# Filter stage, norms, recurrence and routing reordered in a three-block network on one core

## The chip, the cores and the metric

One core of a Trainium2 chip (trn2) runs the whole program once. The time is the device time of that execution in microseconds. The core has five engines that run their own instruction streams and wait for each other by semaphores: TensorE (PE in the rows, its weight loads PEld), VectorE (DVE), ScalarE (ACT), GpSimd (POOL) and SyncE (SP), which here only sends the DMA transfers. TensorE's clock has two levels, 2.4 and 1.2 GHz; the share of the first that was granted stands in the rows as PEclk.

## What is computed

Everything is float32, for 256 tokens of width 1024. Two layers (feed-forward, mixer, feed-forward; the mixers are attention and RWKV-7) are followed by a block with a Hyena and an HGRN2 mixer and a mixture of 16 experts. Each sublayer begins with a norm, modulated by a shift and a scale that come from a conditioning vector:

```python
y = xf * rsqrt(mean(xf * xf, axis=-1) + EPS) * g     # rmsnorm, per token
h = y * (1 + scale) + shift                          # modulate
x = x + factor * gate * _swiglu(h, w_in, w_out)      # silu(h @ w_gate) * (h @ w_up) @ w_down
# second block
h, hc = modulate(rmsnorm(x, g1), ..), modulate(rmsnorm(ctx, g1), ..)
p, pc = h @ w_in, hc @ w_in
y_hy = hyena_mixer(p[..., :1536], ..)     # z = x1 * (h1 conv v); y = x2 * (h2 conv z), filters by their frequencies
y_hg = hgrn_mixer(p[..., 1536:], pc[..., 1536:], ..)
#   S_t = diag(f_t) S_{t-1} + k_t v_t^T,  o_t = S_t^T q_t, both directions, start states from the context
x = x + g1 * concat([rmsnorm(y_hy), readout(y_hg)]) @ w_out
h2 = modulate(rmsnorm(x, g2), ..)
aff = softmax(h2 @ router_w)              # each expert takes its 32 best tokens
x = x + g2 * ec_moe(h2, router_w, w1, w3, w2)        # (silu(xg @ w1) * (xg @ w3)) @ w2, times the gate, added back
return rmsnorm(x, final_g)
```

## The kernel before

**Layout.** Activations lie transposed: 8 tiles of 128 features by 256 tokens (`x3`, `h3`, `sq3`). A float32 matmul is two rows of the trace.

**Norm.** ScalarE squares `x` in four pieces (L1386). TensorE multiplies a 128x128 matrix of ones with each of the eight tiles of squares (L664), so that PSUM bank 7 holds every token's sum in all 128 partitions, and then runs `busy` dummy matmuls on zeros (`keep_clock`, L659). VectorE turns the sums into variances over 128x256 (L1728), ScalarE takes the root (L1374), VectorE the reciprocal (L1724), and eight products with the scale follow (L1731); ScalarE adds the shift (L1391). The norms are numbered: 0 to 5 in the two layers, 6 is the final norm of the first block, 7 and 8 are those of `x` and of the context in the second, 9 is the one ahead of the routing. Norm 0 is special: the first 16 rows of the modulation are dot products on VectorE (`first_dots`, L1757) with weights that are loaded at the start, and GpSimd makes the normalised `x` (L1688).

**Order.** Every engine's program is written out by hand, in the order of the network. SyncE's list is fixed too: a load is sent when the semaphore of its place in the buffer allows, and what stands behind it in the list waits with it. Feed-forward groups are loaded one ahead (gate, up and down weights, 1 MB each), mixer weights go through a ring of four slots of 1 MB (`load`, L592).

**Filter stage.** The frequencies of two Hyena filters are five groups of matmuls each (`filter_freq`, L1039 to L1043) on sums and differences of the two filter sides, which VectorE makes (`filter_sides`) into one pair of buffers; it then empties the banks (`filter_end`, L2079 to L2083). TensorE's order is norm 6, filter 0, norm 7, filter 1, then `b2_in`: 20 of the 22 units of the input projection (L1071, L1069; a unit is 32 rows), with the Hyena convolutions between them. The last two units are cut into pieces of eight rows that `beside(i)` puts between steps of the recurrence (L1084), as it does with the Hyena half of the output projection (L1095).

**Recurrence.** `hgrn` does the scan by doubling: after `level` (L1123, eight matmuls for a direction) at block size 2^lev VectorE `taken`s the new part of the score matrix under a mask (L2126, L2129: two passes of 128x512), scales queries and keys (L2141, L2142) and updates the decays (L2147, L2148). There are eight rounds of two directions, called half levels here. Ahead of it stand turning the Hyena result (`hyena_back`, L1205), turning the context keys (L1108) and the context states (L1115); behind it the crossing between the two token halves (L1143), a last product (L2151), the output sums (L1151 to L1157), their norm, and the rest of the output projection (`b2_out`, L757).

**Routing and experts.** TensorE computes logits (L1215), turns them, the tokens and the affinities, and spreads each expert's row of affinities over 128 partitions (`spread`, L1238). VectorE ranks every token of an expert (`select`, L2222, L2224) and makes the picking matrix of the expert's 32 tokens (`pick`); TensorE gathers them (`picked`, L1247). An expert's weights are 12 loads of 2 MB, 192 in all, through nine places; place n is free when `moe_slot` says so. Loads 2 to 5 wait for the end of the output sums (`hg_out`), load 7 for the output projection, load 8 for the turned tokens, load 9 for the first slot's matmuls:

```python
            sp.wait_ge(sem("hg_out"), 2)
            for n in range(2, 6):
                expert_load(n)
```

## Time and profile before

| | us |
|---|---|
| median of 3 runs | 2678.49 (2677.92 to 2680.62) |
| the profiled execution | 2676.36 |
| its span, first to last instruction | 2674.3 |
| TensorE busy | 2302.1 (86%) |
| VectorE busy | 774.6 (29%) |
| ScalarE busy | 344.9 (13%) |
| chain that ended last: TensorE, DMA, VectorE | 62%, 30%, 7% |
| DMA traffic | 709.51 MB |

The rows come from one profiled execution; times in them count from the start of its span. The chain is followed back from the last instruction through whatever released each step. A busy TensorE is not always on it: in the experts it is busy beside the transfers. Matmuls overlap, so the mean time of one is longer than its share of a group.

### The profile page before, as it was taken

The numbers are of one execution on the slowest core, as the hardware profiler recorded it, in microseconds if no ns is written. First come the engines' busy times: TensorE is split into PE (matmuls) and PEld (weight loads), VectorE is DVE, ScalarE is ACT, GpSimd is POOL, SyncE is SP. The second block draws the span as 40 slices with busy tenths as digits, with TensorE's granted clock in tenths as the row PEclk, the third lists the DMA queues.
The fourth block names the chain that finished last, engine by engine and source line by source line (L and its number), as shares of the span: only waits on it lengthen the run. The fifth ranks groups of instructions, "written<-read, shape, count | busy, mean of one in ns | idle before, by whom it ended". The sixth has DMA issues, their size and how long they took to land.

```text
span 2674.3 us, 34093 instructions
## 1 busy us (share of the span) xinstructions
PE 2302.1 (86%) x14956; PEld 1619.0 (61%) x14968; DVE 774.6 (29%) x1473; ACT 344.9 (13%) x618; POOL 17.5 (1%) x21
## 2 busy tenths in 40 slices
PE   7999989999999999999999999896666666666675
PEld 5888768888888789888886878652121111111221
DVE  5544534574000465511023338640000000000000
ACT  3001222002000232111002211210000000000000
POOL 1000000000000000000000000000000000000000
PEclk9999999999999999999999999988887788887778
DMA  9889235886445240044442223489999999999997
GB/s 394 343 354 379 95 142 226 354 341 256 157 141 204 90 147 20 24 169 148 136 172 78 66 77 115 189 330 428 428 427 428 426 428 427 428 427 427 426 428 338
DMA packets 70098, 709.51 MB, mean 265 GB/s; under 512 B 7776, under 2 KB 7904, under 8 KB 8672
## 3 DMA queue, kind: packets, MB, share of 16 engines
q1 hardware_dynamic: 69984, 707.79, 65.6%
q8 instruction: 96, 1.57, 0.2%
q14 instruction: 18, 0.15, 0.0%
HBM read 706.71 MB, written 1.05 MB: 265 GB/s over the span
## 4 chain that ended last, share of the span: by engine, by line
PE 62%; DMA 30%; DVE 7%; ACT 1%; issue 1%; SPq 0%; DVEq 0%; ACTq 0%
DMA arena<-in_experts 27%; PE ps L691 11%; PE ps L698 11%; PE ps L708 11%; PE ps L757 5%; PE ps L875 4%; PE ps L1071 4%; PE ps L1282 2%; PE ps L1314 2%; DMA ring<-in_experts 2%; PE ps L664 1%; PE ps L1069 1%; PE ps L773 1%; PE ps L1247 1%; PE ps L787 1%
## 5 line engine op out<-in xcount | busy, mean ns | idle before, releaser
L1282 PE MATMUL ps<-arena 128*32 128x512 f32 x1376 | 211.8, 748 | 147.0 <-DMA arena<-in_experts 146.5
L691 PE MATMUL ps<-hT_sq,arena 128*128 128x256 f32 x1376 | 312.1, 380 | 4.1 <-ACT hT_sq L1391 2.9
L708 PE MATMUL ps<-hid,arena 128*128 128x256 f32 x1408 | 311.1, 379 | 0.2 <-DVE hid L1796 0.2
L698 PE MATMUL ps<-hT_sq,arena 128*128 128x256 f32 x1376 | 311.0, 379 | 0.0
L708 PEld LDWEIGHTS ps<-hid,arena 128*128 128x128 f32 x1408 | 267.4, 190 | 36.9 <-issue 0.6
L691 PEld LDWEIGHTS ps<-hT_sq,arena 128*128 128x128 f32 x1376 | 260.5, 190 | 45.5 <-issue 8.5
L698 PEld LDWEIGHTS ps<-hT_sq,arena 128*128 128x128 f32 x1376 | 261.4, 190 | 35.5
L1282 PEld LDWEIGHTS ps<-arena 128*32 128x32 f32 x1376 | 42.4, 124 | 310.6 <-DMA arena<-in_experts 226.0
L1363 ACT ACTIVATE arena<-ps 128x512 f32<-128x512 f32 (+4 forms) x147 | 89.1, 615 | 946.1 <-PE ps L1293 308.5
L1796 DVE TENSOR_TENSOR hid<-sil,ps 128x256 f32<-128x256 f32 x88 | 37.0, 421 | 560.4 <-ACT sil L1415 560.2
L1757 DVE CUSTOM_DVE_ANT_0 hT_sq<-arena 128x1024 f32<-128x1024 f32 x168 | 194.5, 1221 | 0.0
L2249 DVE TENSOR_TENSOR arena<-arena,ps 128x512 f32<-128x512 f32 x16 | 11.0, 688 | 552.4 <-PE ps L1282 552.4
L1314 PE MATMUL ps<-arena 128*32 128x512 f32 x688 | 108.7, 767 | 36.5 <-DMA arena<-in_experts 33.1
L1415 ACT ACTIVATE sil<-ps 128x256 f32<-128x256 f32 x88 | 33.7, 383 | 779.3 <-PE ps L698 778.9
L1282 PE MATMUL ps<-ring,arena 128*32 128x512 f32 x512 | 79.3, 751 | 48.3 <-DMA ring<-in_experts 48.3
L757 PE MATMUL ps<-arena,ring 128*128 128x256 f32 x512 | 111.5, 379 | 2.6 <-DVE arena L1894 1.8
L757 PEld LDWEIGHTS ps<-arena,ring 128*128 128x128 f32 x512 | 97.1, 190 | 17.6 <-DVE arena L1894 2.3
L2256 DVE TENSOR_TENSOR arena<-ps,arena 128x512 f32<-128x512 f32 x16 | 11.1, 692 | 306.4 <-PE ps L1314 306.4
L875 PE MATMUL ps<-arena 64*64 64x64 f32 x2848 | 85.9, 218 | 3.0 <-ACT arena L1363 2.1
L875 PEld LDWEIGHTS ps<-arena 64*64 64x64 f32 x2848 | 84.4, 135 | 3.8 <-ACT arena L1363 2.5
L1314 PEld LDWEIGHTS ps<-arena 128*32 128x32 f32 x688 | 22.4, 128 | 105.7 <-DMA arena<-in_experts 49.0
L1071 PE MATMUL ps<-hT_sq,ring 128*128 128x256 f32 x384 | 83.9, 379 | 0.0
(370 smaller groups left out, 2184.0 us busy)
## 6 DMA issues: line engine op xcount, KB each, us to landing
arena<-in_experts SPq DMA_DIRECT2D x129, 2048.0 KB, 41.1
arena<-in_ada SPq DMA_DIRECT2D x96, 1024.0 KB, 9.7
ring<-in_experts SPq DMA_DIRECT2D x42, 2048.0 KB, 40.9
ring<-in_ring_w SPq DMA_DIRECT2D x51, 1024.0 KB, 5.1
arena<-in_ffn_gate SPq DMA_DIRECT2D x44, 1024.0 KB, 6.5
arena<-in_ffn_up SPq DMA_DIRECT2D x44, 1024.0 KB, 6.2
arena<-in_ffn_down SPq DMA_DIRECT2D x44, 1024.0 KB, 4.8
hT_sq<-in_experts SPq DMA_DIRECT2D x21, 2048.0 KB, 40.4
```

Of the source, the lines that this page charges most:

```text
L691: last = mm(ps[:, ft, 0:T], gate3[:, kt, ft * P:(ft + 1) * P], h3[:, kt, :], start=kt == 0, stop=kt == KT - 1)
L698: last = mm(ps[:, ft, T:2 * T], up3[:, kt, ft * P:(ft + 1) * P], h3[:, kt, :], start=kt == 0, stop=kt == KT - 1)
L708: last = mm(acc(m), down3[:, ft, m * P:(m + 1) * P], hid3[:, ft, :], start=False, stop=True, skip_group_check=True)
L757: last = mm(out_of(m), slot(seq0 + kt // 2)[:, (kt % 2) * D + m * P:(kt % 2) * D + (m + 1) * P], rhs3[:, kt, :], start=(kt == 0 and m % 2 ...
L875: last = mm(ps[r, bank, kt * HD:(kt + 1) * HD], lhs[r, kt, :], rhs[r, :] if len(rhs.shape) == 2 else rhs[r, kt, :], start=start and (stop ...
L1071: last = mm(o, w[:, kt, j * P:(j + 1) * P], src[:, kt, :], start=kt == 0, stop=kt == KT - 1)
L1282: last = mm(ps[32 * n:32 * n + 32, part, :], e_xe[:, kt, :], w[:, (kt % 2) * SLOT + n * 512:(kt % 2) * SLOT + (n + 1) * 512], start=kt == ...
L1314: last = mm(ps[q:q + 32, 3, :], e_hT[:, i, 32 * n:32 * n + 32], w[:, i * D + nn * 512:i * D + (nn + 1) * 512], start=n == 0 and i < 2, sto ...
L1363: return f(dst, src, ACT.Copy)
L1415: f(sil3[:, ft, :], ps[:, ft, 0:T], ACT.Silu).then_inc(sem("silu_ready"), 1)
L1757: nc.vector.tensor_tensor_reduce(buf[:, out_at * D:(out_at + 1) * D], w, c_rows[:, which * D:(which + 1) * D], 1.0, 0.0, ALU.mult, ALU.add ...
L1796: tt_(hid3[:, ft, :], sil3[:, ft, :], ps[:, ft, T:2 * T], ALU.mult).then_inc(sem("hid_ready"), 1)
```

## The change

It has four parts.

1. *Norms.* The sum is made with the tokens on the partitions: each 128x128 piece of squares is the weights, one column of ones moves, and the sums are 128x2. Variance, root and reciprocal run on 128x2. `widen` then multiplies the broadcast column with the identity, which gives every token's factor in all partitions, and the products read it from PSUM. The dummies are split around `widen`. Norms 6 to 8 have none; there `widen` stands inside the filter groups and between projection units. At the start `x`, the vectors and the constants are loaded ahead of the conditioning row, and VectorE makes the normalised `x`, between the first dot products and the rest.
2. *Filters.* Both filters get their own sides, made ahead of the first group's end; the banks are emptied first and the biases added later.
3. *Recurrence.* `hyena_back` moves ahead of the last unit in `b2_in`; the first levels stand ahead of the turned context keys and the states; level 0 needs no scaled keys; the takes of levels 6 and 7 are block copies on ScalarE; pieces of `beside` move behind the levels, into the crossing and the output norm.
4. *Routing.* Only two experts are spread ahead of the first expert and fourteen behind its first four slots; the affinities are copied ahead of the tokens; dummies stand in the gaps; the tables of Exp and Sqrt are loaded early.

The core of the diff:

```diff
-            def norm(i, busy=0):
+            def norm(i, busy=(0, 0)):
+                if i == 7:
+                    pe.wait_ge(sem("x_ready"), 7 * KT)
                 for kt in range(KT):
                     pe.wait_ge(sem("squares"), 4 * i + kt // 2 + 1)
-                    last = mm(norm_sums(i), ones, sq3[:, kt, :], start=kt == 0, stop=kt == KT - 1)
+                    for tt in range(TT):
+                        last = mm(norm_sums[:, tt:tt + 1], sq3[:, kt, tt * P:(tt + 1) * P], ones[:, 0:1],
+                                  start=kt == 0 and tt == 0, stop=kt == KT - 1, skip_group_check=True)
                 last.then_inc(sem("norm_sum"), 1)
-                keep_clock(6, busy)
+                if busy:
+                    keep_clock(6, busy[0])
+                    widen(i)
+                    keep_clock(6, busy[1])
+
+            def widen(i):
+
+                pe.wait_ge(sem("norm_unit"), i + 1)
+                for tt in range(TT):
+                    last = mm(norm_wide[:, tt * P:(tt + 1) * P], norm_unit[:, tt:tt + 1].to_broadcast([P, P]), ident,
+                              start=True, stop=True)
+                last.then_inc(sem("norm_wide"), 1)
...
-                inverse_root(ts(rstd[:, :], norm_sums(i), 1.0 / D, EPS, ALU.mult, ALU.add), rstd[:, :])
+                root(ts(norm_unit, norm_sums, 1.0 / D, EPS, ALU.mult, ALU.add))
+                nc.vector.reciprocal(norm_unit, norm_unit).then_inc(sem("norm_unit"), 1)
+                dve.wait_ge(sem("norm_wide"), i + 1)
...
-            sp.dma_start(c_rows[:, 0:D], a["c_rows"][:, 0:D]).then_inc(sem("c_landed"), 16)
-            first_rows(0, 1)
-            start()
-            first_rows(1, 3)
+            start()
+            sp.dma_start(c_rows[:, 0:D], a["c_rows"][:, 0:D]).then_inc(sem("c_landed"), 16)
+            first_rows(0, 3)
...
-            norm(1, 20)
+            norm(1, (5, 8))
...
-            norm(6, 11)
+            norm(6, None)
             filter_freq(0)
-            norm(7)
+            norm(7, None)
+            keep_clock(0, 5)
             filter_freq(1)
             b2_in()
-            hyena_back()
             hgrn()
             b2_out()
-            norm(9, 10)
+            norm(9, (5, 3))
...
             norm(6, x3, x3, v("final_g", 0, 8), name="x_ready")
             scale_of(144 + 8, v("norm1_g", 0, 8))
+            filter_sides(1)
             filter_end(0)
             norm(7, x3, h3, coef[:, 0:8])
             filter_end(1)
+            filter_bias()
...
+                        if lev < MASKED:
+                            taken(lev, d)
+                        else:
+                            dve.wait_ge(sem("hg_level"), 2 * lev + d + 1)
...
+                for lev in range(MASKED, NLEV + 1):
+                    hb = 1 << lev - 1
+                    for d in range(2):
+                        act.wait_ge(sem("hg_level"), 2 * lev + d + 1)
+                        for tt in range(TT):
+                            src = ps[:, 4 + 2 * d + tt, :].rearrange("p (h s) -> p h s", s=P)
+                            for lo in range(0, P, 2 * hb):
+                                early, late = (slice(lo + hb * i, lo + hb * (i + 1)) for i in ((0, 1) if d == 0 else (1, 0)))
+                                last = copy(g_A[early, d, tt, :, late], src[early, :, late])
+                        last.then_inc(sem("hg_copied"), 1)
...
+                keep_clock(7, 2)
+                pe.wait_ge(sem("e_rows"), 3)
+                spread(range(0, 2))
+                keep_clock(7, 12)
                 pe.wait_ge(sem("e_rows"), 4)
-                spread(range(0, 8))
...
                         if e == 0 and part == 0:
-                            spread(range(8, NE))
+                            spread(range(2, NE))
```

TensorE from the last projection unit into the recurrence. Before, L1205 turns the Hyena result, L1108 the context keys, L1115 is the states, L1123 the levels, L1084 the pieces beside:

```order
L1069 MATMUL ps<-ring,arena 128x256 x16
L1205 MATMUL ps<-con,arena 128x128 x8
L1108 MATMUL ps<-con,arena 128x128 x16
L1084 MATMUL ps<-hT_sq,ring 128x256 x4
L1115 MATMUL ps<-arena 128x128 x16
L1084 MATMUL ps<-hT_sq,ring 128x256 x4
L1123 MATMUL ps<-arena 128x128 x24
L1084 MATMUL ps<-hT_sq,ring 128x256 x4
```

The same stretch of the changed kernel: L1233 turns the Hyena result, L1147 the context keys, L1135 is the states, L1125 the levels, L1103 the pieces beside:

```order
L1233 MATMUL ps<-con,arena 128x128 x8
L1088 MATMUL ps<-ring,arena 128x256 x16
L1125 MATMUL ps<-arena 128x128 x16
L1147 MATMUL ps<-con,arena 128x128 x16
L1125 MATMUL ps<-arena 128x128 x8
L1135 MATMUL ps<-arena 128x128 x8
L1125 MATMUL ps<-arena 128x128 x8
L1135 MATMUL ps<-arena 128x128 x8
L1125 MATMUL ps<-arena 128x128 x8
L1103 MATMUL ps<-hT_sq,ring 128x256 x4
```

The Hyena result is turned one unit earlier, the first levels lead, and the states stand where the first pieces beside stood.

TensorE from the end of the recurrence to the output projection, before (L1143 crossing, L1151 to L1157 output sums, L1163 their mean squares, L659 dummies):

```order
L1123 MATMUL ps<-arena 128x128 x8
L1095 MATMUL ps<-hT_sq,ring 128x256 x4
L1143 MATMUL ps<-arena 128x128 x8
L1151 MATMUL ps<-arena,sil 128x256
...
L1163 MATMUL ps<-hT_sq,con 128x512 x2
L659 MATMUL ps<-zeros 128x512 x8
L757 MATMUL ps<-hT_sq,ring 128x256 x32
```

And now (L1167 crossing, L1177 to L1186 output sums, L1191 mean squares, L1115 pieces beside, L770 output projection):

```order
L1125 MATMUL ps<-arena 128x128 x8
L1115 MATMUL ps<-hT_sq,ring 128x256 x4
L1167 MATMUL ps<-arena 128x128 x4
L1115 MATMUL ps<-hT_sq,ring 128x256 x4
L1167 MATMUL ps<-arena 128x128 x4
L1115 MATMUL ps<-hT_sq,ring 128x256 x4
L1177 MATMUL ps<-arena,sil 128x256
...
L1191 MATMUL ps<-hT_sq,con 128x512
L1115 MATMUL ps<-hT_sq,ring 128x256 x4
L1191 MATMUL ps<-hT_sq,con 128x512
L1115 MATMUL ps<-hT_sq,ring 128x256 x4
L770 MATMUL ps<-hT_sq,ring 128x256 x32
```

Four pieces have moved into the crossing and the mean squares, and the eight dummies are gone.

TensorE in the routing, before (L1223 turns the tokens, L1227 the affinities, L1238 spreads, L1247 and L1250 pick, L1282 is the first expert):

```order
L1223 MATMUL ps<-con,hT_sq 128x128 x16
L1227 MATMUL ps<-con,arena 16x128 x2
L1238 MATMUL ps<-arena,con 128x256 x8
L1247 MATMUL ps<-arena 128x32 x16
L1250 MATMUL ps<-con,arena 128x128 x2
L1282 MATMUL ps<-arena 32x512 x32
L1238 MATMUL ps<-arena,con 128x256 x8
```

And now (L1251, L1255, L1268, L1277, L1280 and L1312 in the same roles, L657 dummies):

```order
L1251 MATMUL ps<-con,hT_sq 128x128 x16
L1255 MATMUL ps<-con,arena 16x128 x2
L657 MATMUL ps<-zeros 128x512 x2
L1268 MATMUL ps<-arena,con 128x256 x2
L657 MATMUL ps<-zeros 128x512 x12
L1277 MATMUL ps<-arena 128x32 x16
L1280 MATMUL ps<-con,arena 128x128 x2
L1312 MATMUL ps<-arena 32x512 x32
L1268 MATMUL ps<-arena,con 128x256 x14
```

Six spreads have moved behind the first four slots of the first expert, and fourteen dummies stand ahead of the picking.

## Rows read from the trace of the kernel before

**Rows 1.** Stretches: start:end, us, busy us by engine, PEclk, DMA share, GB/s

```profile
1745.00:1750.00 5.00, 5.00 (x24) 4.77 (x23) 5.00 (x27) 0.00 (x0) 0.00 (x0) 0.50 0.00 0
...
1850.00:2650.00 800.00, 522.95 (x3206) 154.46 (x3198) 25.06 (x66) 28.17 (x56) 0.00 (x0) 0.80 1.01 427
```

**Rows 2.** Timeline of SyncE and TensorE in the experts: start, us, engine, line, operation

```profile
1756.62 14.38 SPq L597 DMA_DIRECT2D arena<-in_experts  x6
...
1777.12 1.09 PE L1293 MATMUL ps<-con,arena 128*128 128x128 f32 x4 [3.08 <-DVE arena L2249]
...
1788.06 0.33 SPq L597 DMA_DIRECT2D hT_sq<-in_experts  x1
...
2661.93 1.92 PE L1314 MATMUL ps<-arena 128*32 128x512 f32 x16 [1.39 <-DMA arena<-in_experts]
```

**Rows 3.** Stretches at the second feed-forward group and ahead of the attention

```profile
48.00:51.00 3.00, 1.75 (x8) 1.24 (x7) 3.00 (x5) 0.00 (x0) 0.00 (x0) 1.00 0.95 328
...
266.00:267.00 1.00, 0.00 (x0) 0.00 (x0) 1.00 (x4) 1.00 (x4) 0.00 (x0) 1.00 1.06 442
```

**Rows 4.** Timeline of norm 2, TensorE and VectorE

```profile
403.67 3.62 PE L664 MATMUL ps<-hT_sq,con 128*128 128x256 f32 x16
...
407.40 0.42 DVE L1728 TENSOR_SCALAR rstd<-ps 128x256 f32<-128x256 f32 x1 [2.58 <-PE ps L664]
...
408.31 1.75 DVE L1724 RECIPROCAL rstd<-rstd 128x256 f32<-128x256 f32 x1 [0.48 <-ACT rstd L1374]
```

**Rows 5.** Timeline: the nearest rows to the narrow operations

```profile
1594.84 0.20 ACT L1374 ACTIVATE small<-small 128x2 f32<-128x2 f32 x1
1595.07 0.17 DVE L1724 RECIPROCAL small<-small 128x2 f32<-128x2 f32 x1 [1.34 <-ACT small L1374]
...
1789.64 3.76 PE L1247 MATMUL ps<-arena 128*128 128x32 f32 x32
...
1817.20 0.63 PE L1293 MATMUL ps<-con,arena 128*128 128x128 f32 x4 [0.90 <-DVE arena L2249]
```

**Rows 6.** Timeline of the filter stage, up to the first projection unit

```profile
1406.99 3.62 PE L664 MATMUL ps<-hT_sq,con 128*128 128x256 f32 x16
...
1421.67 1.23 DVE L2071 TENSOR_TENSOR arena<-arena 128x1024 f32<-128x1024 f32 x1 [5.00 <-PE ps L1043]
...
1429.03 3.34 PE L1039 MATMUL ps<-arena 128*128 128x512 f32 x4 [4.01 <-DVE arena L2083]
...
1439.08 27.79 PE L1071 MATMUL ps<-hT_sq,ring 128*128 128x256 f32 x128
```

**Rows 7.** Timeline of the recurrence and the output projection

```profile
1612.23 1.04 PE L1205 MATMUL ps<-con,arena 128*128 128x128 f32 x8
...
1625.52 1.29 DVE L2126 TENSOR_TENSOR arena<-ps,con 128x512 f32<-128x512 f32 x2 [5.48 <-PE ps L1123]
...
1636.13 2.02 PE L1123 MATMUL ps<-arena 128*128 128x128 f32 x16 [0.25 <-DVE arena L2142]
...
1688.02 2.07 PE L1143 MATMUL ps<-arena 128*128 128x128 f32 x8 [2.83 <-DVE arena L2142]
...
1692.71 1.19 PE L1151 MATMUL ps<-arena,sil 128*128 128x256 f32 x2 [2.62 <-DVE arena L2151]
...
1710.32 14.08 PE L757 MATMUL ps<-hT_sq,ring 128*128 128x256 f32 x64 [1.76 <-DVE hT_sq L2163]
```

**Rows 8.** Timeline of TensorE from the spreads to the first expert

```profile
1740.24 5.06 PE L1238 MATMUL ps<-arena,con 16*128 16x256 f32 x16 [1.83 <-ACT arena L1363]
1745.23 7.03 PE L1247 MATMUL ps<-arena 128*128 128x32 f32 x32
...
1753.22 8.48 PE L1282 MATMUL ps<-arena 128*32 128x512 f32 x64 [0.47 <-ACT arena L1363]
```

**Rows 9.** Timeline of VectorE: ranking of the last eight experts, first and what follows

```profile
1762.79 0.48 DVE L2222 SCALAR_TENSOR_TENSOR con<-ps,arena,rstd 128x256 f32<-128x256 f32 x1 [8.18 <-PE ps L1238]
...
1774.80 0.19 DVE L2229 TENSOR_TENSOR arena<-arena 128x30 f32<-128x30 f32 x1
```

More of the change, by code:

```diff
@@ L1100, in hgrn, with level, state @@
             def hgrn():
-                pe.wait_ge(sem("hg_gates"), 1)
-                pe.wait_ge(sem("b2_evac"), B2_FIRST)
-                pe.wait_ge(sem("hy_mixed"), 4)
-                for d in range(2):
+                def level(d, kk, qq):
                     for tt in range(TT):
                         for h in range(HGH):
-                            last = tr(ps[:, 4 + 2 * d + tt, h * P:(h + 1) * P], x_k[:, d, h, tt * P:(tt + 1) * P], ident)
-                        last.then_inc(sem("hg_ctx_t"), 1)
-                beside(0)
-                pe.wait_ge(sem("hg_ctx_kt"), 4)
-                for d in range(2):
+                            last = mm(ps[:, 4 + 2 * d + tt, h * P:(h + 1) * P],
+                                      kk[:, d, h, tt * P:(tt + 1) * P], qq(d)[:, h, tt * P:(tt + 1) * P],
+                                      start=True, stop=True)
+                    last.then_inc(sem("hg_level"), 1)
+                def state(d):
+                    if d == 0:
+                        pe.wait_ge(sem("hg_ctx_kt"), 4)
                     for h in range(HGH):
@@ L1386, in norm @@
                     f(sq3[:, 2 * b:2 * b + 2, :], src[:, 2 * b:2 * b + 2, :], ACT.Square).then_inc(sem("squares"), 1)
-                root(rstd[:, :])
+                if i == 0:
+                    act.wait_ge(sem("c_landed"), 16)
+                    f(c_rows[:, 0:D], c_rows[:, 0:D], ACT.Silu).then_inc(sem("c_ready"), 1)
+                root(norm_unit)
+                if i == 9:
+                    f(small[:, 225:226], ones[:, 0:1], ACT.Exp)
                 if shift is not None:
@@ L1581, in hgrn @@
                     f(sq3[:, 2 * b:2 * b + 2, :], g_F[:, 0, 2 * b:2 * b + 2, :], ACT.Square).then_inc(sem("hg_os"), 1)
+                    if b == 0:
+                        f(small[:, 224:225], ones[:, 0:1], ACT.Sqrt)
                 for h in range(HGH):
@@ L2110, in hgrn @@
                 dve.wait_ge(sem("hg_gates"), 2)
[L2112 to L2116 removed]
+                done(cp(g_F, g_f))
                 def sides(d):
@@ L2285, in _ @@
             dve.wait_ge(sem("norm_sum"), 1)
-            root(ts(rstd[:, :], norm_sums(0), 1.0 / D, EPS, ALU.mult, ALU.add))
-            nc.vector.reciprocal(rstd[:, :], rstd[:, :]).then_inc(sem("x_root"), 1)
-            first_dots(2, 2 * NADA)
+            root(ts(norm_unit, norm_sums, 1.0 / D, EPS, ALU.mult, ALU.add))
+            nc.vector.reciprocal(norm_unit, norm_unit).then_inc(sem("norm_unit"), 1)
+            dve.wait_ge(sem("norm_wide"), 1)
+            for kt in range(KT):
+                tt_(x_unit[:, kt, :], x3[:, kt, :], norm_wide, ALU.mult).then_inc(sem("x_scaled"), 1)
+            first_dots(1, 2 * NADA)
             with dve.Fori(0, NG - 1) as g:
```

181 lines of the change are left out of this document (103 added, 78 removed).

## The prediction

> **What bounds the kernel now.** I read the chain of waits first (62% TensorE, 30% DMA), then TensorE's clock and the DMA share by stretches, then the order of time around each edit. The run has two regimes. Up to about 1757 us a chain of TensorE, VectorE and ScalarE steps sets the time, with two exceptions below. From there to the end the loads of the expert weights set it: 800 us at 427 GB/s with every DMA engine busy [rows 1]. SyncE sends load 9 when TensorE has used up the first of nine slots, at 1756.62, and the last load is being multiplied at 2661.93 [rows 2]: 905.3 us for 183 loads, 4.95 us each. Nothing in the change touches that rate. So the end is (the moment at which the first slot is free) + 905 + a tail of 12, and **each edit is worth what it moves that moment**, provided that no gap opens in the stream afterwards. Before that moment DMA stands idle (0 GB/s in 1745 to 1750), so an earlier first slot is worth its full amount.
>
> **Start (norm 0, other order of loads, no GpSimd product): 0 us.** The product moves from GpSimd to VectorE and the dummy matmuls keep TensorE's clock; I work out the last first-layer activation some 2.5 us earlier. But around it DMA is the limit: in 48 to 51 the engines are 95% busy and TensorE waits [rows 3], for the second group's gate weights, and the bytes ahead of those weights are the same in the new order. Bounds: 3 us gained if the gate weights overtake, 2 lost if VectorE, which now makes the product itself, frees the slots of the next loads later. I take 0 because the transfers end last there.
>
> **Norm 1: 0 us.** Same reason: at 266 to 267 TensorE has nothing to do while DMA still moves 442 GB/s, the first ring slots of the attention [rows 3]. A faster norm only lengthens TensorE's wait; a longer low clock behind it may cost up to 1.
>
> **Norms 2 to 5, each -0.8.** Before, VectorE starts the chain at 407.40 (sum to variance) and is done with the reciprocal over 256 columns, 1.75 us, at 410.06: 2.7 us with the handover [rows 4]. On two columns the root costs 0.20 and the reciprocal 0.17 [rows 5], the sum to variance about as much as the latter: 0.7 with the gaps. They are not what ends last now: five dummy matmuls stand ahead of the widening on TensorE, 5 x 0.215 = 1.07, and the widening's four rows take 0.63, as the four rows of 128 columns do in [rows 5]. 1.7 instead of 2.7: -1.0. The sum itself was 16 rows in 3.62 [rows 4]. Now it is 32 rows of one column each, every one with 128 columns of weights. The nearest row has 32 columns and the same weights: 32 rows in 3.76 [rows 5], 0.115 each, so +0.2 with the handling. Reading the result out of PSUM I take at nothing, since two passes over 512 columns that read PSUM take 1.29 [rows 7], no more than their columns ask for. Four norms: **-3.2**. Bounds for a norm: -1.5 (the rows cheaper) to +0.5 (no row shows one column; at half clock the dummies and widening double).
>
> The Trainium skill says that a small matmul's start-to-start has a floor near 25 ns ("TensorE: Matmul & The Clock Gate", the section "Wait — 56ns, not 53.3ns?"). By that figure the last eight rows of each sum would cost an estimated 0.2 us instead of 0.9 and the forecast would be 3.5 us lower; I stay with the 0.115 us row, as each of these matmuls brings its own 128x128 weights.
>
> **Filter stage and norms 6 and 7: -5.4; input projections: +0.7.** Before, TensorE ends the first filter group, does norm 7's sum, and waits 4.01 us for VectorE, which from 1421.67 builds the second filter's sides and empties the banks; the second group starts at 1429.03 at half clock and the projections at 1439.08 [rows 6]. Now the second filter's sides (2.4 us) lie ahead of the first group's end, so the emptying is 3.0 us instead of 7.1 and lies beside norm 7's sum. In order, from norm 6's sum, which ended at 1410.6 [rows 6]: sum done 1410.8, first group to 1412.5, widening, rest to 1419.8, sum of norm 7 to 1423.5, five dummies to 1424.6, group with the widening inside 9.1 us: projections at 1433.7, **-5.4**. Bias additions (3.8 us) are behind that on VectorE and delay only the context load, which is still sent before 1444 and not needed before 1461. In the projections norm 8 costs 0.2 for its rows and 0.5 for the widening: **+0.7**. Bounds of the pair: -6 to -2.
>
> **Recurrence and output projection: -17.0.** All in the old time scale. Turning the Hyena result back (8 rows, 1.04, at 1612.23 [rows 7]) moves ahead of the last projection unit, so TensorE starts the first two levels at 1613.2 instead of waiting for ScalarE's scaling, the context transposes and its state. VectorE takes the first at 1615.2 instead of 1625.52 [rows 7]. It then does: take and multiply to 1617.1, wait for the transposes (1618.6), ones, copy, multiply to 1620.5, the same for the other direction to 1624.1, take and two products of level 1 to 1626.7. Level 1 starts at 1626.8 instead of 1636.13: **-9.3**. From 1636.13 to 1688.02 lie 13 half levels, 3.99 each, VectorE-bound (five passes: 1.2 + 0.6 + 3 x 0.72); TensorE needs 2.02 + 1.80 - 0.2 = 3.65 of each for a level and its piece beside. Ten such steps stay. In levels 6 and 7 the takes (1.34 each half level) go to ScalarE, whose small copies fit in 3.65, and VectorE falls under TensorE's 3.65: four half levels. The crossing halves carry a piece beside, 0.9 + 1.75 each, and the last product no longer waits for the crossing. Output sums start at 1679.3 instead of 1692.71 [rows 7], **-4.1** more. They took 11.4, the first half at half clock behind two waits of VectorE; with no wait ahead, 8.8: **-2.6**. Then square, mean, two pieces beside, and the first normalised head at 1693.3 instead of 1710.32: **-1.0**. Sum -17.0. SyncE's last weight load and the first two expert loads are sent some 7 us later relative to the levels; they end 15 us before they matter. Bounds: -19 to -9 (ScalarE's copies, which no row shows in 32-partition pieces, or its latency putting a half level above 4.0).
>
> **Norm 9, routing, first slot: -8.2.** Norm -0.8. Copying the turned affinities ahead of the 2.1 us copy of the tokens lets the first two spreads start at 1738.05 instead of 1740.24 (eight spreads, 5.06 us, up to the picking at 1745.23 [rows 8]). One expert is ranked by 1742.0, and the picking starts there: **-2.4**. Picking took 7.03 at half clock [rows 8], granted 0.50 [rows 1], where the same 32 rows take 3.76 at full clock [rows 5]: **-3.3**, if the fourteen dummies hold the clock. The first slot at half clock took 1756.62 - 1753.22 = 3.4, at full 1.75: **-1.65**. Bounds: -9 to -2.5 (clock still low).
>
> **Expert 0, what the routing edit pushes behind it: +1.5.** Ranking takes 12.0 us for eight experts [rows 9], 1.50 each. Fourteen now wait for the spreads behind the first four slots, and the first expert's product stands behind all of them on VectorE. With q the first slot's start: ranking from q + 8.1 to q + 28.9, 2.4 for the selection, TensorE's turn at q + 31.2, and 10.94 (1777.12 to 1788.06 [rows 2]) to the next load, q + 42.2. The eight loads sent meanwhile last from q + 1.9 to q + 41.5: a gap of 0.7, where before 8 us were to spare (1756.62 + 39.6 = 1796.2 against 1788.06). TensorE idles 11 us there and restarts at half clock: up to 1.7 more. I take +1.5. Bounds 0 to +4.
>
> **Sum:** 0 + 0 - 3.2 - 5.4 + 0.7 - 17.0 - 8.2 + 1.5 = -31.6. The profiled execution took 2676.36 (span 2674.3): 2644.8, a span of 2642.7. The median of the runs is 2.1 above it: **2646.9**.
>
> **Rivals.** (a) *The low clock stays*, behind idle in the recurrence's end and in routing: the 2.6 + 3.3 + 1.65 above are not gained, 2654.5. For it: routing still has gaps between short steps (the stretch after them was granted 0.50). Against: 14 dummies in those gaps. The Trainium skill ("TensorE: Matmul & The Clock Gate", Part 1) calls the half clock the default that only activity lifts; the 0.50 of 1745 to 1750 agrees. (b) *ScalarE or TensorE paces the recurrence*: 6 us less, 2653. (c) *The start follows the compute after all*: 3 more, 2644. (d) *The gap in the expert stream is larger*, 4 more, 2651. (e) *Slower: narrow sums at the cost of a wide matmul.* 7 norms before the first slot count (2 to 7 and 9), 224 one-column rows. The whole gain of 31.6 is gone when a row costs 0.14 us more than the 0.115 taken, from 0.26 us on; at 0.38, the mean of a wide row, it is 59 us: 2706. Half clock would give 0.22 (7.03 / 32), a gain of only some 8 us: 2670. Against: 0.115 is already with a full weight load.
>
> **How the numbers follow.** Forecast 0.50, (a) 0.18, (b) 0.10, (c) 0.10, (d) 0.07, (e) 0.05, of which 0.03 slower. Range 2640 to 2660: from the forecast with (c) and cheap rows together, to (a) with 5 of (b) or (d); it leaves out (e) and combinations, about 0.1. What this kernel's measurement can tell from no change is about 0.2%, 5 us. Faster 0.95, same 0.02, slower 0.03.
>
> **What the profile after would show.** The first layer's second group still at 49 to 50 and the attention still starting at 267 (else the start's zero is wrong); 1.7 us from a norm's sum to the first product; projections about 8.6 earlier than 1439; the level steps 4.0 for ten and 3.65 after; output sums at full clock in 8.8; picking 3.7 us long; the first expert load behind the first slot near 1723.5, and at most a 2 us dip in DMA some 41 us after it. Wrong in kind would be a low clock in the layer behind each norm, or DMA idle in the experts.

## The result, and where the time went

| us | before | after |
|---|---|---|
| median | 2678.49 (2677.89 to 2680.62) | 2663.38 (2662.35 to 2665.5) |
| profiled execution | 2676.36 | 2662.74 |
| its span | 2674.3 | 2661.0 |

The change makes the kernel 15.1 us faster, a ratio of 0.9946 (95% interval 0.9933 to 0.9959). The forecast was 31.6 and 2646.9, its range ended at 2660: right in sign, wrong by half. In the spans, 13.3 us were gained.

The first question is at which moments the two executions part. The start of a TensorE step in both timelines gives this; each line is the length of a stretch, after minus before:

| stretch (from, to) | forecast | measured |
|---|---|---|
| start to norm 2's sum (403.67, now 401.53) | 0 | -2.1 |
| norms 2, 3, 4, 5, sum to what follows it | -3.2 | +2.0, +0.4, +0.2, -1.2: +1.4 |
| feed-forwards and RWKV between them | 0 | +1.4 |
| filter stage (sum of norm 6 to projections) | -5.4 | -0.85 |
| input projections, norm 8 among them | +0.7 | +5.55 |
| recurrence, up to the output projection | -17.0 | -18.1 |
| norm 9, routing, first slot | -8.2 | -5.8 |
| first slot to last slot of the experts | +1.5 | +2.6 |
| behind the last slot | 0 | +2.7 |
| sum | -31.6 | -13.3 |

The largest item, the recurrence, is right to 1.1 us. What failed are the terms in which a norm's sum stands: norms 2 to 5, the filter stage and the projections. The timeline of TensorE in the changed kernel at norm 2 (start, us, engine, line, operation, operands, shapes, count) shows why; it answers to [rows 4]:

```profile
401.53 4.48 PE L665 MATMUL ps<-con,hT_sq 128*128 128x1 f32 x32
406.25 1.91 PE L657 MATMUL ps<-zeros 128*128 128x512 bf16 x4 [0.24 <-issue]
407.95 1.06 PE L677 MATMUL ps<-con,small 128*128 128x128 f32 x4
408.81 1.06 PE L657 MATMUL ps<-zeros 128*128 128x512 bf16 x2
...
411.15 3.62 PE L704 MATMUL ps<-hT_sq,arena 128*128 128x256 f32 x16
```

and the stretches of it (start:end, us, busy us of TensorE, its weight loads, VectorE, ScalarE, GpSimd, then granted clock, DMA share, GB/s):

```profile
403.00:404.00 1.00, 1.00 (x11) 1.00 (x11) 0.00 (x0) 0.98 (x2) 0.00 (x0) 1.00 0.00 0
404.00:405.00 1.00, 1.00 (x7) 1.00 (x7) 0.00 (x0) 0.57 (x1) 0.00 (x0) 0.54 0.00 0
405.00:406.00 1.00, 1.00 (x5) 0.97 (x7) 0.00 (x0) 0.00 (x0) 0.00 (x0) 0.50 0.00 0
406.00:410.00 4.00, 3.76 (x12) 2.04 (x11) 1.27 (x5) 0.64 (x3) 0.00 (x0) 0.50 0.00 0
...
411.00:412.00 1.00, 1.00 (x6) 0.89 (x5) 1.00 (x4) 1.00 (x4) 0.00 (x0) 1.00 0.00 0
```

TensorE counts as fully busy, with one-column rows, and its clock falls from 2.4 to 1.2 GHz (granted 1.00, then 0.50) in the middle of them. In the same norm of the kernel before, the clock is 1.00 throughout:

```profile
403.00:406.00 3.00, 3.00 (x15) 2.64 (x15) 1.82 (x6) 2.45 (x4) 0.00 (x0) 1.00 0.00 0
406.00:411.00 5.00, 4.26 (x19) 2.16 (x19) 3.08 (x5) 1.52 (x3) 0.00 (x0) 1.00 0.00 0
```

The rest of the sum, the dummies (1.91 us, 1.24 where the clock holds) and the widening (1.06, then 0.61) pay for it, and then whatever comes next until it is back: in the filter stage and in the projections those are wide matmuls on the path. The timeline there, answering to [rows 6]:

```profile
1407.58 3.68 PE L665 MATMUL ps<-con,hT_sq 128*128 128x1 f32 x32
1411.13 3.60 PE L1052 MATMUL ps<-arena 128*128 128x512 f32 x4
...
1421.88 4.27 PE L665 MATMUL ps<-con,hT_sq 128*128 128x1 f32 x32
1426.39 1.92 PE L657 MATMUL ps<-zeros 128*128 128x512 bf16 x4 [0.24 <-issue]
1428.09 3.58 PE L1052 MATMUL ps<-arena 128*128 128x512 f32 x4
...
1438.82 27.79 PE L1090 MATMUL ps<-hT_sq,ring 128*128 128x256 f32 x128
1467.82 5.89 PE L665 MATMUL ps<-con,hT_sq 128*128 128x1 f32 x32 [1.21 <-ACT hT_sq L1417]
1473.57 9.97 PE L1090 MATMUL ps<-hT_sq,ring 128*128 128x256 f32 x32
```

Four rows of L1052 should take 1.88; behind both sums they take 3.6. Norm 8's sum takes 5.89 instead of 3.7 and the unit behind it 9.97 instead of 7.0: those two are the 4.9 us missing in the projections.

The recurrence and the routing, as [rows 7, 8]:

```profile
1631.70 2.02 PE L1125 MATMUL ps<-arena 128*128 128x128 f32 x16 [0.28 <-DVE arena L2196]
...
1683.55 0.60 PE L1177 MATMUL ps<-arena,sil 128*128 128x256 f32 x2
...
1697.54 13.98 PE L770 MATMUL ps<-hT_sq,ring 128*128 128x256 f32 x64
...
1730.34 3.73 PE L1277 MATMUL ps<-arena 128*128 128x32 f32 x32 [0.30 <-DVE arena L2307]
1734.79 8.77 PE L1312 MATMUL ps<-arena 128*32 128x512 f32 x64 [0.47 <-ACT arena L1394]
```

From the first levels at 1618.39, the half level that stood at 1636.13 comes 13.3 us later (forecast 13.6), the output sums 51.85 behind it (52.5), the output projection 14.0 behind those (14.0). The picking takes 3.73 instead of 7.03, as forecast.

In the experts the DMA stream has a dip some 41 us behind the first slot; two stretches of it, DMA share and GB/s at the end:

```profile
1775.00:1780.00 5.00, 5.00 (x50) 3.39 (x52) 0.00 (x0) 0.41 (x1) 0.00 (x0) 1.00 0.81 341
1780.00:1785.00 5.00, 5.00 (x49) 3.86 (x42) 0.00 (x0) 0.00 (x0) 0.00 (x0) 1.00 0.89 301
```

Against 427 GB/s that is (86 + 126) x 5 / 427 = 2.5 us lost. And the end of the run is at half clock (3.78 for the last eight rows), where in the kernel before it was at full clock (1.99 for the same rows):

```profile
2645.91 2.97 PE L1344 MATMUL ps<-arena 128*32 128x512 f32 x16 [2.97 <-DMA arena<-in_experts]
2649.68 3.78 PE L1353 MATMUL ps<-arena 64*128 64x512 f32 x8 [0.79 <-DVE arena L2321]
```

### The profile page after: what moved, and what is told of

It reads as the page before. It is cut to its first block, busy times and chain, and to the rows that moved or that the text cites. A ratio compares the mean times of both kernels' runs of the same rounds, so it can differ in the third digit from the quotient of the medians.

```text
span 2661.0 us, 34512 instructions
## 1 busy us (share of the span) xinstructions
PE 2324.3 (87%) x15163; PEld 1638.8 (62%) x15176; DVE 746.1 (28%) x1470; ACT 348.1 (13%) x633; POOL 5.2 (0%) x13
## 4 chain that ended last, share of the span: by engine, by line
PE 63%; DMA 30%; DVE 6%; issue 1%; ACT 0%; SPq 0%; DVEq 0%; ACTq 0%
DMA arena<-in_experts 26%; PE ps L704 11%; PE ps L711 11%; PE ps L721 11%; PE ps L770 5%; PE ps L1090 4%; PE ps L888 4%; PE ps L1312 2%; PE ps L1344 2%; DMA ring<-in_experts 2%; PE ps L665 1%; PE ps L1277 1%; PE ps L1088 1%; DMA arena<-in_ada 1%; DMA ring<-in_ring_w 1%
## 5 line engine op out<-in xcount | busy, mean ns | idle before, releaser
L1312 PE MATMUL ps<-arena 128*32 128x512 f32 x1376 | 231.4, 811 | 144.2 <-DMA arena<-in_experts 143.7
L1312 PEld LDWEIGHTS ps<-arena 128*32 128x32 f32 x1376 | 44.8, 131 | 319.4 <-DMA arena<-in_experts 225.1
L1394 ACT ACTIVATE arena<-ps 128x512 f32<-128x512 f32 (+7 forms) x159 | 92.5, 591 | 913.1 <-PE ps L1323 322.3
L1344 PE MATMUL ps<-arena 128*32 128x512 f32 x688 | 114.3, 807 | 36.7 <-DMA arena<-in_experts 32.5
L1312 PE MATMUL ps<-ring,arena 128*32 128x512 f32 x512 | 83.1, 783 | 49.4 <-DMA ring<-in_experts 49.4
L770 PE MATMUL ps<-arena,ring 128*128 128x256 f32 x512 | 111.5, 380 | 1.5 <-DVE arena L2072 0.8
L770 PEld LDWEIGHTS ps<-arena,ring 128*128 128x128 f32 x512 | 97.2, 190 | 16.4 <-DVE arena L2072 1.3
```

Of the source, the lines that this page charges most:

```text
L770: last = mm(out_of(m), slot(seq0 + kt // 2)[:, (kt % 2) * D + m * P:(kt % 2) * D + (m + 1) * P], rhs3[:, kt, :], start=(kt == 0 and m % 2 ...
L1312: last = mm(ps[32 * n:32 * n + 32, part, :], e_xe[:, kt, :], w[:, (kt % 2) * SLOT + n * 512:(kt % 2) * SLOT + (n + 1) * 512], start=kt == ...
L1344: last = mm(ps[q:q + 32, 3, :], e_hT[:, i, 32 * n:32 * n + 32], w[:, i * D + nn * 512:i * D + (nn + 1) * 512], start=n == 0 and i < 2, sto ...
L1394: return f(dst, src, ACT.Copy)
```

## The experiments

All medians are of 4 executions beside the kernel before on the same chip (2678.0 to 2678.6), of 9 where it says so.

### The columns of the norm sums

Theory N says that the one-column rows let the clock fall; its rival W, that the waits and the fewer dummies behind them do.

**128 columns.**

```diff
-last = mm(norm_sums[:, tt:tt + 1], sq3[:, kt, tt * P:(tt + 1) * P], ones[:, 0:1],
+last = mm(ps[:, 7, tt * 128:(tt + 1) * 128], sq3[:, kt, tt * P:(tt + 1) * P], ones[:, 0:128],
```

> The changed kernel with one edit: in the norm sums the moving operand is 128 columns of ones instead of one (the sums are read from every 128th column). Theory N: the 32 one-column rows of a norm sum use TensorE so little that its clock falls to half at their end (granted 1.00 at 403 to 404, 0.50 from 405 to 410 in the changed kernel), and what follows pays for it. A row of 128 columns costs the same 0.113 us (32 rows in 3.73 in the recurrence), so the sums stay 3.6 us long, the clock stays at 1.00, and the gains are: norm 2 from sum to first product 9.6 -> 6.4 (-3.2), norm 3 8.0 -> 6.4 (-1.6), norm 4 -1, filter stage -4.8, norm 8 and the projections behind it -5.1, norm 9 -1.5: -17, a median near 2646 (2644 to 2650). Rival W: the clock falls because of the waits and the fewer dummies behind the sum (5 and 2 instead of 10), not because of its columns: nothing changes, 2663, and the stretches behind the norms stay at 0.50.

Measured: 2648.7 (2647.6 to 2650.1), ratio 0.9887 [0.9871, 0.9904]; 14.7 us below the changed kernel. The same places, norm 2 first:

```profile
406.27 3.73 PE L666 MATMUL ps<-con,hT_sq 128*128 128x128 f32 x32
409.84 1.24 PE L658 MATMUL ps<-zeros 128*128 128x512 bf16 x5
410.92 0.61 PE L678 MATMUL ps<-con,small 128*128 128x128 f32 x4
...
412.73 1.53 PE L705 MATMUL ps<-hT_sq,arena 128*128 128x256 f32 x6
```

```profile
1406.99 3.73 PE L666 MATMUL ps<-con,hT_sq 128*128 128x128 f32 x32
1410.57 1.88 PE L1053 MATMUL ps<-arena 128*128 128x512 f32 x4
...
1424.25 1.88 PE L1053 MATMUL ps<-arena 128*128 128x512 f32 x4
...
1433.28 2.97 PE L1091 MATMUL ps<-hT_sq,ring 128*128 128x256 f32 x13
...
1462.27 3.84 PE L666 MATMUL ps<-con,hT_sq 128*128 128x128 f32 x32 [1.20 <-ACT hT_sq L1418]
1465.95 7.07 PE L1091 MATMUL ps<-hT_sq,ring 128*128 128x256 f32 x32
```

128 times the columns take 0.1 us more (3.73 against 3.63 for 32 rows), and what follows runs at full clock. W falls: the waits and the number of dummies are the changed kernel's. Sum of norm 2 to first product is 6.46 instead of 9.62, the filter stage 26.3 instead of 31.2, and the first slot is free 37.8 us behind the start of the output projection instead of 40.5. (The clock at norm 2 is 1.00 from 406 to 412.) In the two profiled executions norms 2 to 5 and 9, the filter stage and the projections give 17.3 us; 4.7 of it is lost again in the attention (139.25 instead of 134.60), whose own code is the same in both.

**32 columns.** The same edit with 32 in place of 128.

> As the run with 128 columns, but 32 columns of ones. N: the picking's rows have 32 columns, ran at full clock (3.73 for 32) and had a first slot at half clock behind them, so 32 columns should hold the clock less well than 128: a time between the two, 2650 to 2661, with 0.50 left behind some of the norms. W: 2663.

Measured: 2655.8, with the widest scatter of the first four kernels (2650.3 to 2659.6); between the two, as N says. In its profile the clock is low behind the sums of norms 1 to 3, 6, 8 and 9 and stays up behind 4, 5 and 7 (timeline of the filter stage, norm 6 and norm 7):

```profile
1410.11 3.66 PE L1053 MATMUL ps<-arena 128*128 128x512 f32 x4
...
1425.49 1.88 PE L1053 MATMUL ps<-arena 128*128 128x512 f32 x4
```

**Part 1 undone.** The core of the edit, in the changed kernel:

```diff
-                    for tt in range(TT):
-                        last = mm(norm_sums[:, tt:tt + 1], sq3[:, kt, tt * P:(tt + 1) * P], ones[:, 0:1], ...)
+                    last = mm(norm_sums, ones, sq3[:, kt, :], start=kt == 0, stop=kt == KT - 1)
...
-                widen(i)
```

> The changed kernel with its norms undone, all else kept: 16 rows of 256 columns against the ones, variance, root and reciprocal over 128x256, the dummies in one row (26, 20, 10, 10, 18, 10, and 10 for norm 9), no widening. What part 1 is worth inside the changed kernel. N: the clock holds, norm 2 7.6 instead of 9.6, norm 3 -0.4, norm 4 -0.2, norm 5 +1.2, norm 8 and behind it -5.5, norm 9 -0.3, filter stage -5.7 by the clock and the missing widening but +2 to +3 for the 1.75 us reciprocals that come back on VectorE: about -10, 2653. W: the longer row of dummies holds the clock too, the same; but if the narrow norms are not what costs the time, undoing them costs 0.8 to 1.0 each on VectorE: 2668.

Measured: 2649.6 (2649.3 to 2650.7), 13.8 us below the changed kernel, 3.4 below the 2653 expected. So part 1 as written costs 13.8 us of what the other parts bring, and even with its clock held it is worth 0.9, less than the scatter. The 2 to 3 us that I expected from the long reciprocals in the filter stage didn't come: projections start 25.15 behind norm 6's sum. In the profile the four norms of the layers do cost 1.14 each more than with 128 columns, but the widening and a stall in RWKV (below) are gone, and its attention is 3.0 us shorter with the same code, so the 0.9 is not a clean price.

**Dummies inside the sums.**

```diff
+                    if kt % 2 == 1 and kt < KT - 1:
+                        keep_clock(0 if i == 7 else 6, 2)
```

> The changed kernel with its one-column sums kept, and two dummy matmuls (512 columns, 0.215 us each) behind the 8th, 16th and 24th row of every norm sum. It asks whether it is the missing work on TensorE, and nothing else in the one-column rows (their PSUM writes, the read of them), that makes the clock fall. Theory N: with 1.3 us of dummies in each sum the clock stays at 1.00 behind the sums, as with 128 columns; each sum is up to 1.3 us longer, of which the ones that wait for squares hide a part: seven norms on the path, 0.5 to 1.3 each, so 14.7 gained less 4 to 9: 2653 to 2658. Rival: something else in the narrow rows does it: the clock still falls behind the sums and the dummies come on top, 2667 to 2672.

Measured: 2663.3 (9 executions, 2660.4 to 2673.2), no change, between the two forecasts. The profile splits: the clock holds at norms 4 to 7 and 9, where the filter stage takes 28.3 us instead of 31.2, and still falls at norms 1, 2, 3 and 8 (stretches at norm 2, then the timeline behind norm 6's sum):

```profile
404.00:406.00 2.00, 2.00 (x13) 1.57 (x12) 0.00 (x0) 0.82 (x1) 0.00 (x0) 0.73 0.00 0
406.00:408.00 2.00, 2.00 (x11) 1.72 (x10) 0.16 (x1) 0.01 (x1) 0.00 (x0) 0.50 0.00 0
```

```profile
1415.61 1.96 PE L1054 MATMUL ps<-arena 128*128 128x512 f32 x4
```

So more work between the narrow rows may help (in the changed kernel the clock fell at eight of these nine norms, here at four), but one execution of each is weak evidence where the clock also differs without an edit; this much is not a sure cure, and it costs what it saves. Theory N has its support from the run with 128 columns, with the 32 columns in between. What in a one-column row lets the clock fall is not shown.

### The gap in the expert stream

**Six experts spread first.**

```diff
-                spread(range(0, 2))
-                keep_clock(7, 12)
+                spread(range(0, 6))
+                keep_clock(7, 4)
...
-                            spread(range(2, NE))
+                            spread(range(6, NE))
```

> The changed kernel with six experts spread ahead of the first expert in place of two (the four spreads stand where eight of the twelve dummies stood), ten behind the first four slots in place of fourteen. Theory G: the DMA stream's dip at 1775 to 1785 (341 and 301 GB/s, 2.5 us lost) comes from fourteen rankings that stand ahead of the first expert's product on VectorE; with ten, 6 us less stand there, and the dip is gone: -2.5, 2661, with the picking still starting some 4 us behind the first spread. Rival: the dip has another cause (the half clock of the turns and of the row constants) and stays: 2663; or the spreads take longer than the dummies and push the picking back by up to 1 us: 2662.

Measured: 2664.5 (2659.6 to 2667.0), no gain, for a reason that I had not listed. The dip is gone, and from load 9 to the last slot's matmuls pass 905.24 us (1744.91 to 2650.15) instead of 907.87; theory G holds. But with eight dummies fewer the picking is at half clock, which costs 3.3, and the norms of this execution differ from the changed kernel's with the same code (norm 5 takes 9.57 instead of 6.38, norm 9 8.66 instead of 7.79) (TensorE's timeline; then the stretch where the dip was):

```profile
1733.25 7.00 PE L1277 MATMUL ps<-arena 128*128 128x32 f32 x32 [0.19 <-DVE arena L2307]
```

```profile
1780.00:1785.00 5.00, 5.00 (x47) 3.41 (x40) 0.00 (x0) 0.00 (x0) 0.00 (x0) 1.00 1.00 419
```

**No dummies in the routing** (both `keep_clock(7, ...)` taken out, on top of the 128 columns).

> The kernel with 128-column sums (2648.7) without the fourteen dummies between the routing's steps (2 ahead of and 12 behind the first two spreads). The clock there: with the dummies it is granted 1.00 from 1700 to 1730. If they hold it, the picking runs at half clock as in the kernel before (7.0 instead of 3.73) and the first slot too (3.3 instead of 2.0): +4.6, 2653. Rival: the clock holds without them, since TensorE is kept busy up to 2 us before: 2648.7, and the dummies are idle weight.

Measured: 2651.4 (2651.2 to 2653.3), +2.7. In the profile load 9 is sent 15.8 us behind the first spread instead of 10.6, +5.2, near the 4.6 forecast. Why the median shows half of it is not settled. The clock differs here without an edit as well: in the profile of the run with takes on VectorE (below), which keeps all fourteen dummies, the picking took 4.8 and load 9 was sent 13.6 behind the first spread, so this one profile may overstate what the dummies are worth on average. TensorE's picking and first slots:

```profile
1715.11 7.00 PE L1276 MATMUL ps<-arena 128*128 128x32 f32 x32 [3.00 <-DVE arena L2306]
...
1723.07 9.18 PE L1311 MATMUL ps<-arena 128*32 128x512 f32 x64 [0.47 <-ACT arena L1393]
```

**Four experts first** (two, five dummies, two more, five dummies; twelve behind), on top of the 128 columns.

> The kernel with 128-column sums (2648.7) with the first of the joined kernel's two edits alone: four experts spread ahead of the first expert, no dummies in the last one. It parts the 4.9 us. By the two traces the DMA gap behind the first slots gives 1.75 (907.7 to 906.0 from load 9 to the last slot's matmuls) and the last expert 3.3 (15.7 to 12.4 behind them), but the latter was at full clock in some kernels without any dummies: 2647 by this; 2644 if the last expert's dummies do nothing; 2648.7 if the spreads do nothing.

Measured: 2643.1 (2640.4 to 2648.5). Load 9 to the last slot takes 905.24 again, and the picking 3.65: the gap is closed without losing the clock. 5.6 us by the medians is more than the 2.5 of the gap. The two profiled executions lie 9.0 apart, and there it can be told: 2.5 are the gap, 3.0 the attention (136.29 instead of 139.25) and 3.3 the end behind the last slot (12.4 instead of 15.7). The code of the last two is the same in both kernels, so only the 2.5 can be put down to the edit.

### ScalarE's copies in the recurrence

On top of the 128 columns, the takes of levels 6 and 7 go back to VectorE:

```diff
-        MASKED = 6
+        MASKED = 8
```

> The kernel with 128-column sums (2648.7), with the takes of levels 6 and 7 back on VectorE (masked copies, 1.34 a half level), all else of the recurrence kept. My working says VectorE is under TensorE in these half levels only because ScalarE copies: four half levels of 3.5 (two measured at 1671.29 and 1674.80, 3.51 apart, then the crossing) become 4.0, and the last product ahead of the output sums waits 1.34 longer twice: +2 to +4.5, 2651 to 2653. Rival: ScalarE's copies bought nothing, TensorE's pieces beside set the pace anyway: 2648.7.

Measured: 2650.4 (2647.9 to 2653.5), +1.7, within the scatter, so the median doesn't decide. In the profile the path from the first levels to the output sums is 68.37 instead of 65.17: +3.2, with the late half levels 4.0 apart and TensorE waiting ahead of the second crossing half, as forecast:

```profile
1665.64 1.13 PE L1168 MATMUL ps<-arena 128*128 128x128 f32 x8 [0.25 <-DVE arena L2197]
...
1669.94 1.16 PE L1168 MATMUL ps<-arena 128*128 128x128 f32 x8 [1.45 <-DVE arena L2197]
```

### A version that beats both

**Joined**: 128 columns, four experts first, and dummies in the last expert:

```diff
                         last.then_inc(sem("moe_slot"), 1)
+                        if e == NE - 1:
+                            keep_clock(2, 6 if n < 3 else 3)
```

> The kernel with 128-column sums (2648.7) and two more edits. (1) Four experts are spread ahead of the first expert, the second two between two rows of five dummies, twelve behind the first four slots: 3 us of ranking less stand ahead of the first expert's product, the DMA gap of 2.4 us there closes, and the dummies keep the picking at full clock, unlike the run with six spreads, whose picking took 7.0. (2) In the last expert six dummies (three behind the last slot) stand behind each of the last four slots' matmuls, while TensorE waits for the loads, so that the last products run at full clock (1.99 instead of 3.78 for the last eight rows, and 1.9 instead of 3.4 for the last slot): up to -2.7. Together -2 to -5: 2644 to 2647. Rival: the dummies in the last expert stand in the way of a slot whose load has landed while the clock is still low (6 x 0.43 = 2.6 on top of 3.4): +1 to +2 and no gain.

Measured: 2643.8 (2641.9 to 2645.2), ratio 0.9869 [0.9853, 0.9885]. The end of its profile runs at full clock:

```profile
2631.09 1.92 PE L1347 MATMUL ps<-arena 128*32 128x512 f32 x16 [1.57 <-DMA arena<-in_experts]
...
2633.83 1.99 PE L1358 MATMUL ps<-arena 64*128 64x512 f32 x8
```

Without the last expert's dummies (the run above) the median is 0.7 lower and the scatter 8 us instead of 3.4, with a profiled end that was at full clock too: that they gain anything in the median is not shown.

**More dummies in the attention**, on top of that:

```diff
-            norm(1, (5, 8))
+            norm(1, (5, 21))
...
+                keep_clock(6, 8)
                 pe.wait_ge(sem("mla_c"), 4)
```

> The joined kernel (2643.8) with thirteen more dummies behind norm 1 (21 in place of 8, 2.8 us more, in the 3.09 us in which TensorE waits for the attention's first weights) and eight more ahead of the attention's own norm (1.7 us, in a wait of 1.99 for ScalarE). The granted clock in the attention differs from execution to execution of the same code: 0.59 in 268 to 272 and 0.61 in 292 to 296 in the joined kernel, 1.00 throughout in the changed one. If the idle ahead of them is the cause, both stretches are at 1.00 now, and the attention (sum of norm 2 minus its first product) takes 134.6 as in the changed kernel instead of 138.0: up to -3.4 in the profile, 1 to 3 in the median: 2641 to 2643, with less scatter. Rival: the fall has another cause and stays: 2643.8.

Measured: 2640.25 (2639.6 to 2641.0), ratio 0.9859 [0.9843, 0.9875]: 38 us below the kernel before, 23 below the changed one, with a scatter of 1.4 us. The two stretches in the joined kernel, then in this one:

```profile
268.00:272.00 4.00, 4.00 (x12) 3.21 (x12) 4.00 (x7) 1.32 (x1) 0.00 (x0) 0.59 0.01 4
292.00:296.00 4.00, 4.00 (x12) 3.01 (x12) 0.09 (x1) 0.94 (x1) 0.00 (x0) 0.61 1.01 428
```

```profile
268.00:272.00 4.00, 4.00 (x21) 3.51 (x20) 4.00 (x7) 1.32 (x1) 0.00 (x0) 1.00 0.03 8
292.00:296.00 4.00, 3.76 (x18) 1.50 (x16) 2.82 (x4) 0.63 (x1) 0.00 (x0) 1.00 1.02 430
```

The attention, up to norm 2's sum, takes 134.6 instead of 138.0, the number expected, and both stretches are at 1.00: with the idle filled the fall is gone, as the theory had it. Not all of the 3.6 us in the median need be the attention's: in the profile the stall in RWKV (below) is gone as well, which is 1.2.

## Why the prediction was wrong, step by step

**Norms 2 to 5: the step that failed.** This term said -3.2 and measured +1.4. The mechanism on VectorE is right: three steps on two columns, and with the clock held 1.14 gained per norm (0.8 forecast). The price of a row is right as well: 32 one-column rows take 3.63, 0.113 each, as long as the clock holds. What failed is the step from a row's price to the norm's: the sum prices the rows for their own time alone and takes the work behind them at full clock. What I left out is what such rows do to the engine's clock. I priced the row by its nearest neighbour and wrote half clock only as a bound for the dummies and the widening of these four norms (+0.5 each; norm 2 came to +2.0). In rival (e) I worked out half clock for the sums' own rows as a 2670 case. In neither did I carry it to the work behind the sums. (The 2706 beside it is too high: 0.38 is the mean duration of overlapping rows; a wide row's share of its sum is 3.62 / 16 = 0.226.) The sentence in the prediction that should have stopped me is in its last part: it names a low clock behind each norm as what would make it wrong in kind, and gives it no chance.

**Filter stage and projections: the sums are right, the clock under them is not.** With 128 columns they come to -5.8 and +0.57, against -5.4 and +0.7 in the prediction and -0.85 and +5.55 in the changed kernel. Here alone 9.4 of the missing 18 us lie. Norms 2 to 5 are 4.6 more, and norm 9 (+0.3 instead of -0.8) another 1.1. The first slot at half clock (3.25 instead of 1.75) is 1.5 more, but it is not the narrow rows' doing, see the routing. The Trainium skill ("TensorE: Matmul & The Clock Gate", Part 1), which I weighed in rival (a) for the routing only, calls half clock the default that only activity lifts. The 0.50 at 405 to 410 agrees as to the level, but the fall to it came while the profile shows TensorE busy all the time, from 403 to 406.

**Start and norm 1: 0 forecast, -2.1 measured.** The second feed-forward group starts at 49.58 and the attention at 266.93, so the DMA bound holds there, as said. 0.4 us of the 2.1 lie ahead of the attention and 1.7 in it (134.60 instead of 136.29), and those come from the clock, by a detour. Behind norm 1's one-column sum it fell (0.59 from 260 to 264), the dummies and the widening took longer, and TensorE waited only 1.48 us for the first weights instead of 2.31. The attention then started at full clock. With 128 columns the clock holds at the norm, the wait is longer and the fall comes in the attention (before, changed, 128 columns):

```profile
267.38 22.64 PE L773 MATMUL ps<-hT_sq,ring 128*128 128x256 f32 x96 [2.31 <-ACT hT_sq L1391]
```

```profile
266.93 20.96 PE L786 MATMUL ps<-hT_sq,ring 128*128 128x256 f32 x96 [1.48 <-DMA ring<-in_ring_w]
```

```profile
267.02 23.99 PE L787 MATMUL ps<-hT_sq,ring 128*128 128x256 f32 x96 [3.10 <-DMA ring<-in_ring_w]
```

The prediction gave a low clock behind this norm up to 1 us of loss; it gave back 1.7, which is luck in the forecast's favour.

**RWKV: nothing forecast, +1.7.** 1.5 of it is one stall; see below.

**Recurrence: -17.0 forecast, -18.1 measured.** Every step of it held to 0.7 us. Two slips in the working did no harm: 1636.13 is the start of level 2, not 1, and of the twelve half levels behind it the text counts ten at 4.0 and four at 3.65, while its 1679.3 comes of ten and two. Measured were nine steps of 4.0 and three of 3.5 to 3.6. ScalarE's copies, the uncertain part, are worth 3.2 in the profile.

**Routing: right but for norm 9 and the clock of the first slot.** The earlier spreads and the ranking of one expert gave 2.3 (2.4 forecast), the picking 3.3 (3.3). In the profile with 128 columns norm 9, routing and first slot together give -8.5 against -8.2. But the first slot at full clock is not owed to the columns: it took 1.99 there and in the run with four experts first, and 3.27 with the wide norms and 3.47 in the joined kernel, where the clock behind norm 9 held too. With the fourteen dummies the picking ran at full clock in five of six profiled executions; that they hold it for the first slot, as the term of -1.65 assumes, is not borne out.

**Experts: +1.5 forecast, +2.6 measured, and +2.7 at the end.** The gap was of the kind forecast (a gap of 0.7 and up to 1.7 by the clock) and is 2.5; it goes when fewer rankings stand ahead of the first product. The half clock at the very end I took as 0, as the kernel before had it full there. That it is the change's doing is not shown: kernels with the same code at the end took 3.78 for the last eight rows in five profiled executions (the changed one, 128 and 32 columns, six experts first, no routing dummies) and 1.99 in four (wide norms, dummies in the sums, takes on VectorE, four experts first).

With 128 columns the first slot is free at 1724.84, where the prediction's sum says 1723.5. The forecast's time, 2646.9, is near what the change gives without its narrow rows (2648.7), not what it gives. Even that nearness is partly luck: in its profile, at 2650.1, the attention and the end cost 3.0 and 3.4 us that the forecast doesn't have, and the norms, the filter stage and the recurrence give part of it back.

## What to carry to other kernels

A step that replaces wide matmuls by narrow ones must be priced twice: for its own time, and at either clock for everything on the path behind it, since a TensorE that the profile shows fully busy can still lose its clock. Where a row's time is nearly the same at 1 and 128 columns, as here, take the wide one, also when 127 results are thrown away. A step made shorter ahead of a wait lengthens the wait, and what stands behind it may then start at the lower clock. A profile is one execution: where the clock differs without an edit, compare a stretch in several kernels that share its code before giving its change to an edit. Where the time behind such a step matters, look first at the granted clock by short stretches, before looking for waits; and when dummies are traded for real but small work, look at it again.

## What the runs showed of the hardware

- 32 float32 matmul rows with 128x128 weights take 3.63 us with one moving column, 3.66 with 32 and 3.73 with 128. With one column the granted clock fell to 0.50 at or behind the sums of norms 0 to 4 and 6 to 9 of the profiled execution and stayed 1.00 behind norm 5; in the run with six experts first, with the same norms, it fell behind norm 5 as well. With 128 columns it stayed 1.00 behind the sums of norms 0 to 9.
- The first 96 rows of the attention took 22.4 to 24.0 us in the seven profiled executions in which TensorE had waited 2.2 to 3.1 us ahead of them, and 20.9 to 21.0 in the five in which it had waited 0 to 1.5. The same code at the same place got different clocks: behind waits of 3.0 to 3.1 us the attention took 136.1, 136.1, 136.3, 138.0 and 139.3 us in five kernels that share it. Filled waits made it 134.6.
- RWKV has one stall of 1.5 us on TensorE in which nothing that the profile shows was waited for, at the same matmul in the changed kernel and in seven of the others, and in neither the kernel before, nor the one with its norms undone, nor the one with dummies inside the sums, nor the last one. In the changed kernel:

```profile
1010.06 3.31 PE L888 MATMUL ps<-arena 64*64 64x64 f32 x106 [1.50 <-issue]
```

What decides it was not tried and stays open; TensorE's program differs in length between these kernels.
